# Later gathers, pooled semaphore clears and a half-first start of the recurrence in a two-layer block

## The reference, cut to what matters

```
layer 0 mixer: latent attention + gated linear attention
layer 1 mixer (rglru):
  branch, rnn = split(h_lat @ w_in); rnn_c = h_ctx @ w_in[:, 1280:]
  rnn = dwconv(rnn); r, i = sigmoid gates per block of 128 channels
  log_a = -8 * softplus(-lambda) * r;  x_in = sqrt(1 - exp(2 log_a)) * (i * rnn)
  y = forward scan + backward scan, started from the context's final state
  out = (gelu(branch) * y) @ w_out
feed-forward (peer), each layer:
  idx, g = top 16 of 128*128 experts per head, 8 heads
  act = gelu(h . u[idx]);  out = sum(g * act * v[idx])
```

## Time and profile before

| | |
|---|---|
| median of three runs | 4595.95 us (4595.48 to 4604.45) |
| the profiled execution | 4595.48 us |
| its span, first to last instruction | 4593.7 us |
| mean granted TensorE clock | 0.94 of full |
| PE busy | 4057.2 us, 88% |
| DVE busy | 2969.0 us, 65% |
| barriers of all engines at L61 | 31 |

### The profile page before, as it was taken

One profiled execution on the slowest core, in us unless ns is written; L12 is line 12 of the kernel. 1 busy time (PEld: TensorE's weight loads), 2 busy tenths in 40 slices (PEclk: granted clock), 3 DMA queues, 4 the chain that ended last, 5 costly groups with the idle time before them and its releaser, 6 DMA issues. The chain is left out here.

```text
span 4593.7 us, 71028 instructions
## 1 busy us (share of the span) xinstructions
PE 4057.2 (88%) x23644; PEld 2191.2 (48%) x23644; DVE 2969.0 (65%) x8221; ACT 1538.9 (33%) x1944; POOL 1450.3 (32%) x1073
## 2 busy tenths in 40 slices
PE   5898777999999999699999986877998797699996
PEld 1555563656556556344444441433555454444442
DVE  2036445165565565688888875773298888588887
ACT  0015220034444444222222211880154354333332
POOL 0500000411111111266666640210413233267774
PEclk8989878999999999899999998988999898899998
DMA  5100340356887887699999975112489999999996
GB/s 213 63 27 1 76 148 13 102 163 182 218 237 184 218 238 197 238 344 349 340 346 345 340 258 184 57 48 78 145 220 292 321 340 302 324 327 344 346 346 224
DMA packets 374059, 1003.03 MB, mean 218 GB/s; under 512 B 34944, under 2 KB 121792, under 8 KB 366528
## 3 DMA queue, kind: packets, MB, share of 16 engines
q1 hardware_dynamic: 208332, 522.43, 32.6%
q0 software_dynamic: 100512, 317.24, 24.4%
q10 hardware_dynamic: 64996, 160.55, 9.3%
HBM read 804.43 MB, written 146.90 MB: 207 GB/s over the span
## 5 line engine op out<-in xcount | busy, mean ns | idle before, releaser
L1449 PE MATMUL ca_A<-hh,ca_uh 128*128 128x512 f16 (+2 forms) x3072 | 794.0, 313 | 106.2 <-DVE ca_ul L1543 50.8
L1449 PE MATMUL ca_A<-hl,ca_uh 128*128 128x512 f16 (+2 forms) x3072 | 793.2, 313 | 0.0
L1449 PE MATMUL ca_A<-hh,ca_ul 128*128 128x512 f16 (+2 forms) x3072 | 792.7, 312 | 0.0
L1409 POOL DMA_DIRECT2D ca_ul<-ca_ur x186 | 165.4, 889 | 1137.1 <-ACT ca_ul L1482 1093.7
L1974 PE MATMUL ex_R<-ex_vh,ex_wh 128*128 128x512 f16 x1280 | 486.1, 380 | 36.0 <-DVE ex_wl L1988 36.0
L1974 PE MATMUL ex_R<-ex_vl,ex_wh 128*128 128x512 f16 x1280 | 486.1, 380 | 0.0
L1974 PE MATMUL ex_R<-ex_vh,ex_wl 128*128 128x512 f16 x1280 | 486.0, 380 | 0.0
L1449 PEld LDWEIGHTS ca_A<-hh,ca_uh 128*128 128x128 f16 x3072 | 261.3, 99 | 299.2 <-DVE ca_ul L1543 55.7
L1490 ACT ACTIVATE ca_ga<-ca_A 128x640 f32<-128x640 f32 (+1 forms) x256 | 152.9, 597 | 665.3 <-PE ca_A L1449 608.3
L1449 PEld LDWEIGHTS ca_A<-hh,ca_ul 128*128 128x128 f16 x3072 | 261.6, 99 | 195.1 <-issue 12.6
L2202 PE MATMUL ex_R<-ex_vh,ex_wh 128*128 128x512 f16 x768 | 293.3, 382 | 68.3 <-DVE ex_wl L2216 34.2
(11 more groups left out here) (378 smaller groups left out, 7685.4 us busy)
## 6 DMA issues: line engine op xcount, KB each, us to landing
ca_ur<-in_peer_u SPq DMA_DIRECT2D x256, 512.0 KB, 5.3
ex_vr<-in_peer_v SPq DMA_DIRECT2D x256, 512.0 KB, 7.5
gates<-ca_stage ACTq DMA_DIRECT2D x32, 2048.0 KB, 11.3
ca_ul<-ca_ur POOLq DMA_DIRECT2D x186, 256.0 KB, 5.5
acts<-ca_ga ACTq DMA_DIRECT2D x128, 320.0 KB, 2.9
ex_gr<-gates SPq DMA_DIRECT2D x32, 1280.0 KB, 7.7
ex_ar<-acts SPq DMA_DIRECT2D x128, 320.0 KB, 5.1
acts<-ca_ga ACTq DMA_DIRECT2D x128, 192.0 KB, 6.0
```

The source lines that it names most:

```text
L1409: nc.gpsimd.dma_start(ul[j][:, :, :].rearrange("p k n -> p (k n)"), ur[j][:, :, :].rearrange("p k n -> p (k n)"), accum_op=ALU.add).then_i ...
L1449: last = nc.tensor.matmul(A[b][:, a:a + w], lhs[j][:, k, :], rhs[:, k, a:a + w], start=(k == 0 and x == 0), stop=(k == KD - 1 and x == 2))
```

## The change

Three edits.

1. `signals` no longer clears on exit. Its semaphores go to a list RETIRED; they are cleared together, with one barrier, only when a stage asks for more names than are free, and once at the very end. The barrier that ends each Block stays.
2. In both second products POOL waits for `weighed >= GC + 1`, which is the first weighing of activations (the counter is set to GC beforehand), before its first gathers: 8 of them in layer 0, 4 in layer 1.
3. `decay_rates` goes into `rglru`: its stage is gone, its load, two ACT functions and DVE operations stand at the start of the recurrence. The first block's weights are loaded as two halves, b=1 first, with a semaphore of its own. Every cast and every subtraction now handles b=1 first, each half of `pl` has its own count in `wp_cut`, and PE's `near` waits for b=1 only, the branch for b=0. For the first block DVE subtracts instead of POOL.

```diff
 def signals(nc, *names):
     stage = next(STAGE)
+    if len(nc.free_semaphores) < len(names):
+        clear_retired(nc)
+        nc.all_engine_barrier()
     sems = [nc.alloc_semaphore(f"{n}_{stage}") for n in names]
     yield sems
-    nc.clear_and_free_semaphores(sems)
-    nc.all_engine_barrier()
+    RETIRED.extend(sems)
+def clear_retired(nc):
+    nc.clear_and_free_semaphores(list(RETIRED))
+    RETIRED.clear()
...
                     pool.wait_ge(index_set, 1)
+                    pool.wait_ge(weighed, GC + 1)
                     for x in range(SLOTS):
                         gather(u_rows, ug, x, 0, ug_in)
...
+                    first = io["od_w_in"][0].rearrange("p (b k m) -> p b k m", b=2, k=KD)
+                    for b in (1, 0):
+                        sp.dma_start(wp[0][:, b], first[:, b]).then_inc(wp_in[0] if b == 0 else first_in, 16)
+                    sp.dma_start(lam[:, :, :], io["od_lambda"]).then_inc(lam_in, 16)
                     sp.dma_start(rates[:, :, 4:13], io["od_consts"].rearrange("n p m -> p n m")).then_inc(cn_in, 16)
-                    for j in range(2):
-                        load(j, j, True, True)
+                    load(0, 0, False, True)
+                    load(1, 1, True, True)
                     with sp.Fori(1, RG_N // 2) as it:
                         for j in range(2):
-                            sp.wait_ge(wp_cut, it * 2 + (j + 1))
+                            sp.wait_ge(wp_cut, it * 4 + (2 * j + 2))
...
                 def _(pool):
+                    def low(it, j):
+                        for x, b in enumerate((1, 0)):
+                            pool.wait_ge(wp_high, it * 4 + (2 * j + x + 1))
+                            nc.gpsimd.tensor_tensor(pl[j][:, b], wp[j][:, b], ph[j][:, b], ALU.subtract).then_inc(wp_cut, 1)
+                    pool.sem_inc(wp_cut, 4)
+                    pool.wait_ge(wp_cut, 6)
+                    low(0, 1)
...
                     def near(m, j):
-                        pe.wait_ge(wp_cut, m * 2 + (j + 3))
+                        pe.wait_ge(wp_cut, m * 4 + (2 * j + 5))
...
                     def branch(m, j):
+                        pe.wait_ge(wp_cut, m * 4 + (2 * j + 6))
...
-                        for b in range(2):
+                        for b in (1, 0):
                             nc.scalar.activation(ph[j][:, b], wp[j][:, b], ACT.Copy).then_inc(wp_high, 1)
...
-                    for j in range(2):
-                        cast(0, j)
+                    cast(0, 0)
+                    act.wait_ge(lam_in, 16)
+                    step(nc.scalar.activation(dx[:, :, :], lam[:, :, :], ACT.Abs))
+                    nc.scalar.activation(dx[:, :, :], dx[:, :, :], ACT.Exp, scale=-1.0).then_inc(exped, 1)
+                    cast(0, 1)
...
                     step(nc.vector.memset(z[1][:, :], 0.0))
+                    dve.sem_inc(y_done, 2)
+                    for x, b in enumerate((1, 0)):
+                        dve.wait_ge(wp_high, x + 1)
+                        nc.vector.tensor_tensor(pl[0][:, b], wp[0][:, b], ph[0][:, b], ALU.subtract).then_inc(wp_cut, 1)
+                    dve.wait_ge(lam_in, 16)
+                    decay_rates()
                     dve.wait_ge(cn_in, 16)
-                    dve.sem_inc(y_done, 2)
...
         peer(nc, io, mods, dram, H, HS, hh, hl, ident, 1, CTX_TILES, True, True, out=out)
+        clear_retired(nc)
+        nc.all_engine_barrier()
```

More of the change, by code:

```diff
@@ L51 @@
 STAGE = count()
+RETIRED = []
 @contextmanager
@@ L2271, in _ @@
                     period(NG - 1, 1, False)
[L2274 to L2312, removed]
 def rglru(nc, io, hh, hl, MIX, rates, early):
@@ L2324, in rglru @@
         sb = lambda n, s: c.enter_context(nc.sbuf_tensor(f"rg_{n}", s, F32))
+        lam, dx, ds, du, dp = (sb(n, [P, RG_N, 2]) for n in ("lam", "dx", "ds", "du", "dp"))
         wp = [sb(f"wp{j}", [P, 2, KD, P]) for j in range(2)]
@@ L2338, in rglru @@
         with signals(nc, "wp_in0", "wp_in1", "wg_in0", "wg_in1", "proj", "copied", "conv", "gate", "sig", "decayed",
-                     "squared", "rooted", "y_done", "own", "aown", "wp_cut", "wp_high", "cn_in", "branch_done") as (
-                wp_in0, wp_in1, wg_in0, wg_in1, proj, copied, conv, gate, sig, decayed, squared, rooted, y_done, own, aown, wp_cut, wp_high, cn_in, branch_done):
+                     "squared", "rooted", "y_done", "own", "aown", "wp_cut", "wp_high", "cn_in", "branch_done", "first_in", "lam_in", "exped", "rated") as (
+                wp_in0, wp_in1, wg_in0, wg_in1, proj, copied, conv, gate, sig, decayed, squared, rooted, y_done, own, aown, wp_cut, wp_high, cn_in, branch_done,
+                first_in, lam_in, exped, rated):
             wp_in, wg_in = (wp_in0, wp_in1), (wg_in0, wg_in1)
@@ L2378, in _ @@
                 def _(pool):
-                    pool.sem_inc(wp_cut, 2)
-                    with pool.Fori(0, RG_N // 2) as it:
+                    def low(it, j):
[5 more added lines that the diff above has]
+                    low(0, 1)
+                    with pool.Fori(1, RG_N // 2) as it:
                         for j in range(2):
-                            for b in range(2):
-                                pool.wait_ge(wp_high, it * 4 + (2 * j + b + 1))
-                                ins = nc.gpsimd.tensor_tensor(pl[j][:, b], wp[j][:, b], ph[j][:, b], ALU.subtract)
-                            ins.then_inc(wp_cut, 1)
+                            low(it, j)
                 @block.tensor
@@ L2427, in cast @@
                     def cast(m, j):
-                        act.wait_ge(wp_in[j], m * 16 + 16)
+                        if isinstance(m, int) and m * 2 + j == 0:
+                            act.wait_ge(first_in, 16)
+                        else:
+                            act.wait_ge(wp_in[j], m * 16 + 16)
                         act.wait_ge(branch_done, m * 2 + (j + 1))
-                        for b in range(2):
+                        for b in (1, 0):
+                            if isinstance(m, int) and m * 2 + j + b == 0:
+                                act.wait_ge(wp_in[0], 16)
                             nc.scalar.activation(ph[j][:, b], wp[j][:, b], ACT.Copy).then_inc(wp_high, 1)
```

19 lines of the change are left out of this document (18 added, 1 removed).

## The result

| | before | after |
|---|---|---|
| median, runs taken side by side | 4599.59 us (4593.62 to 4604.45) | 4575.77 us (4570.75 to 4583.77) |
| the profiled execution | 4595.48 us | 4575.41 us |
| its span | 4593.7 us | 4573.6 us |
| mean granted TensorE clock | 0.94 | 0.944 |

The ratio is 0.9949, 95% interval 0.9939 to 0.9960: faster by 18 to 28 us. The forecast was 39 us faster, 4556.5 us, with a range up to 4571; the kernel came out above that range.

A forecast was written before the change was run, and what follows sets the result against it. PE was taken as busy nearly throughout, so gains had to come from stretches where it stands still. Terms 11 + 13 + 3 + 9 + 3 = 39 us off 4595.5 gave 4556.5 us, range 4544 to 4571.

The forecast's parts named there:

- Pooled clears: At stage exits: four barriers stay of 31, a longer clear for each; 11 us gained (8 to 16).
- The recurrence's start: At the recurrence's start: PE's first product comes at 2848.3 in place of 2861.26; 13 us gained (11 to 14).
- its cover: At the recurrence's start: moved decay chain and subtractions lie beside PE's first work, each with 4 us or so to spare.
- Inside the recurrence: In the recurrence's loop: `near` waits for one subtraction, so PE starts earlier each period; 3 us gained (0 to 7).
- the quarter of it: In the recurrence's loop: a quarter of PE's remaining 12.9 us wait for POOL taken as gain, 3 us.
- that chain: In the recurrence's loop: ACT, the fuller engine, needs its gelu behind MIX, which waits for DVE's scan and POOL, not PE.
- Later gathers, layer 0: Layer 0's second products: PE starts 10.3 us sooner, group two's last activations land 6 us earlier; 9 us gained (2 to 10.3).
- PE's first group: Layer 0's second products: first group takes 25.9 + 2.6 us, until 1931, so the second starts at 1932.2, not 1941.4.
- Later gathers, layer 1: Layer 1's second products: PE comes 5 us earlier, group two's last activations 4 us earlier; 3 us gained (-1 to 5).
- Rival (d): Layer 1's second products: the loop settles at about 18.5 us a group, not 16.7, costing 54 us, 4610 in all; chance 0.03.
- Rival (a): Both second products: delayed gathers give nothing lasting, since transfers are conserved; without their 12 us, 4568; chance 0.15.

The follow-up runs named there:

- Run 1: The kernel before with only the pooled semaphore clears: 4582.97 us, ratio 0.9970.
- Runs 3 and 6: The kernel before with only the recurrence edit, 4583.8 us; the changed kernel with `near` waiting for both low halves again, 4579.02 us.
- run 7: The changed kernel with ten spare products of 256 columns behind each branch, into a bank nobody reads: 4576.35 us, ratio 0.9950.
- runs 8 and 9: The changed kernel with DVE, not POOL, subtracting the recurrence's low halves: behind MIX, 4735.27 us; in mid block behind the first direction's i*cv, 4588.41 us.
- run 4: The changed kernel with each group's activations loaded ahead of its values and weights cast before values, both second products: 4556.19 us, ratio 0.9920.

## Why the prediction was wrong, point by point

- **Pooled clears: right.** 10.4 us (the decay's exit apart) beside 11. The count of four was right, a name costs what was said; that the names form several ranges with a drain each was missed and cost under 1 us. Run 1 has it alone.
- **The recurrence's start: right in its sum, with luck in its cover.** 12.5 us beside 13. The decay chain was hidden, but with 0.36 us to spare and not 4. Counted from the stage's first load it was to end at 9 to 11 us and ended at 17.4. Two things made it late: its DVE operations stood behind the second half's cast and subtraction and began only at 9.95, and POOL stretched them by 3.8, which the prediction did allow for. It stayed hidden because the projection was late as well: its rg_Z copies, which the first convolution needs, were to be ready after 15.1 us and were ready at 17.6.
- **Inside the recurrence: wrong, and out of its bounds.** 3 us (0 to 7) were expected, and it lost 1.4 between the two traces and 0.4 to 2.0 between any two of the eight that have the old or the new loop and no other edit in it. PE's 12.9 us of waiting went as foreseen, to 1.6; the quarter of it that was to come off the stage did not, since the gate products behind the projection wait for ACT, and ACT for MIX. The prediction named that chain and then priced a share against it. Runs 3 and 6 show the idle time moving; run 7 speaks against the clock as the cause, though it mended the clock only in part. Which engine sets the loop's pace no run settles: runs 8 and 9 take POOL's interference away and pay more for it on DVE. The stretch of DVE's operations by POOL is in both kernels (MIX 1335 ns on average after, 1333 before), so it is no part of the difference.
- **Later gathers, layer 0: this is the step that failed most.** The mechanism up to PE's first product was right to 0.3 us. The sentence that failed is "the last activations 1 us earlier at 1918.5 ... 6 us earlier": they came 1.5 us earlier. Counted from the stage's first load the weighing was to come at 36.8 us and came at 41.3. The queue was taken as full from 1897.5 on, which is 15.7 us after that load; in fact SP waits to reload until the first weights are cut, and POOL's first gather is only being issued, so that for about 4 us the transfers carry 51 GB/s, and they are full again from 1893.5, 18.2 us after the load. That is 2.5 of the 4.5 us. From 1893.5 to 1916.0 they moved 8.64 MB at 384 GB/s, where the sum had 406: another 1.2 us. The rest, under 1 us, is open. These shares are read from the trace; no run takes the pause away. What the prediction did not ask is whether the activations need to stand among SP's values, which nobody needs so soon. The weighings are 4.5 us apart for 0.85 MB, 188 GB/s, with the gathers taking the other half of the transfers: from 1900 to 1908 SP's queue moved 1.50 MB and the gathers' 1.79. The Trainium skill (DMA: Bandwidth & Descriptors, section "Queues, rings and completion order") gives just this: an engine goes round its queues packet by packet. The trace agrees. The prediction drew from it that the order between gathers and loads does not matter, and did not look at the order within SP's own queue, which does: run 4, which turns that order and ACT's casts with it, gets 7.4 us, under the same pause.
- **PE's first group** was to take 28.5 us and took 35.3. It began before group two's supply was there, stopped for 4.67 us when the four banks were full, and went on at the lower clock. Even without that stop group two could start only when POOL was done, at 1930.2, 0.9 us sooner.
- **Later gathers, layer 1: nothing that can be told.** 1.1 us beside 3 in the two traces, within its bounds (-1 to 5), but the executions with and without the wait overlap. PE's first product came 5.4 us sooner, as forecast. Group two's last activations were weighed 1.2 us sooner in the two traces and not 4, and at 30.3 to 31.5 us after the load without the wait, 30.3 to 31.8 with it, over nine: the pause and the shared transfers again. Rival (d) did not come: the period after the first is 18.6, then 16.7 us.
- **The rest.** In the two traces 12.7 us of the 39 did not come. A further 6.2 us of the distance is stages whose code is the same, most of it one that scatters by 12 us between executions. Rival (a), at 4568 with a chance of 0.15, was nearest: of the gathers' 12 us 4.8 lasted, layer 1's part of it within scatter. The range lacked the case that loop and gathers both fall short, and it held nothing for scatter, though it was worked out against one execution.

## What to carry to other kernels

Moving a transfer out of the way moves its bytes into the next stretch. Work out which load ends that stretch's wait and where it stands in its queue; here the later gathers were worth 3 us or so in layer 0 until the activations were put ahead of the values, and 11 with it. When a wait of one engine is taken away in a pipelined loop, follow the chain to the next wait of the same engine before any of it is counted; if it ends in an engine that is as full as before, the gain is nothing. Before a difference of a few us between two traces is explained, look at how far the same code scatters over other executions; here that took away a gain of 1.1 us and half of a loss of 6.6. A short operation that changes engine takes its place in that engine's order with it: one subtraction behind the last operation of a block cost 158 us, in the middle of the block 17.

## What the runs showed of the hardware that was not expected

- A clear of pooled names is not one instruction: nine range clears for four clears, each after a drain of POOL of 59 to 260 ns. They take 44 to 810 ns and 2.7 us together; the longest is the one clear before the recurrence, which by the prediction's count has 143 names.
- A DVE copy, with one input only, is also stretched beside POOL's subtractions: 1.34 us at 2912.52 and 0.17 at 2938.02, POOL being busy from 2911.40 to 2915.91 and only until 2937.10. The copy ended at 2913.86, just as the first of POOL's two subtractions did (2913.83). Two more blocks of this trace show the same (1.35 and 1.36 us, ending 0.02 and 0.03 us behind a subtraction), and the seven copies that meet no subtraction take 0.17 or 0.18.

```profile
2911.40 4.51 POOL L2357 TENSOR_TENSOR rg_pl<-rg_wp,rg_ph 128x1024 f16<-128x1024 f32 x2 [18.06 <-ACT rg_ph L2416]
...
2912.52 1.34 DVE L2469 COPY rg_cn<-rates 128x15 f32 x1 [0.67 <-DVE MIX L2512]
...
2938.02 0.17 DVE L2469 COPY rg_cn<-rates 128x15 f32 x1 [0.38 <-DVE MIX L2512]
```
